# A Mamba-2 SSD stretch between two MLPs on one Trainium2 core: its order rewritten unit by unit, with steps moved between engines

## The chip, the cores and the metric

The kernel runs on one core of one Trainium2 chip. Its engines are TensorE (PE in the rows; PEld is its weight load), VectorE (DVE), ScalarE (ACT) and GpSimd (POOL), and SyncE (SP), whose queue issues nearly all DMAs. Each engine works through its own instructions in program order and meets the others at semaphores. The metric is the device time of one execution in microseconds.

## The reference, cut to what matters

512 tokens of width 1024 go through two layers: a pooling mixer with an MLP, then the SSD mixer with an MLP. The change touches the SSD mixer alone:

```python
zxbcdt = h @ w_in                       # z 2048, xBC 3072, dt 32
xbc = silu(causal_dwconv(xbc, conv_w, conv_b))      # 4 taps
dt = softplus(dt_raw + dt_bias); a = -exp(a_log)
# per group g of 4 (8 heads of 64, state 128), per chunk c of 128 tokens:
a_cs = cumsum(dt * a)
decay = exp(a_cs[l] - a_cs[s]) for s <= l
y_diag = (C B^T * decay) @ (x * dt)
y_off = (C @ state) * exp(a_cs);  state = state * exp(a_cs[-1]) + B^T @ (decay_to_end * x * dt)
y = (y_diag + y_off + d_skip * x) * silu(z)
y = y * rsqrt(mean over the group of y*y + eps) * norm_g
return y @ w_out
```

## The kernel before, in words

Activations lie feature-major: 128 features on the partitions, 512 tokens along them. Every large product is done in "units": one unit is a 1024 x 128 block of weights, eight weight tiles, and for each three matmuls of 512 columns (lines 696 to 698: high part by high, high by low, low by high), 24 in all, into one PSUM bank. A unit's weights are loaded by SP into one of two `w_raw` buffers; ACT rounds each half into `w_hi` (`round_half`, line 373) as soon as TensorE has used the same half of the unit two before; GpSimd subtracts (`split_half`, line 571) to get `w_lo`; SP may then load the unit after the next into `w_raw`. Two PSUM banks in turn are the accumulators.

The SSD stretch is 57 units. The first, a "slot" each from here on, gives the raw dt; six more give B, C and four x tiles of group 0. Then each group has ten slots t = 0 to 9: t = 0 to 3 are its four z tiles, t = 4 to 9 the six conv tiles (B, C, four of x) of the next group. In group 3, the slots from t = 4 on are the 16 units of the output projection instead; the first eight use groups 0 and 1, the last eight (from t = 12) groups 2 and 3.

Between units TensorE does the small matmuls of the group, at places fixed by tables: transposes of x and B and the products of C and B (`token_major`, lines 826, 829, 832) after t = 0, the four chunks (`chunk`, lines 845, 852, 858: diagonal part, state part, new state) after t = 2, 4, 6, 8 (2, 4, 5, 6 in group 3), the statistic of the previous group's squares (line 731) after t = 4 and its spread over the partitions by a product of ones and diagonals (line 738) after t = 5. In group 3 both are done once more at the end, the spread in the middle of the unit of slot t = 10.

On VectorE the conv of a tile is a load out of PSUM times the token's rstd (`conv_load`, line 1059, into `conv_in`), then four taps (lines 1073 and 1077), with Silu on ACT (line 477) behind them, tile by tile. The decay of a chunk is broadcast from DRAM into `m`; VectorE subtracts (line 1140) and limits (line 1146), ACT takes Exp (line 510), VectorE multiplies by the masked C B product (`decay_times_cb`, line 1153). Behind a chunk VectorE adds and decays y and state (lines 1162 to 1190). Of the group's norm VectorE does the diagonals (line 952, from `make_diagonals`, behind ACT's square root, line 403), the product with rstd and gain (line 1218) and the rounding (line 1226), GpSimd the sum of squares (line 645) and the residue (line 652). Elsewhere, in the MLPs, lines 1014 and 1018 are the square of the hidden tile and its residue.

The order on each engine is written out by hand in that engine's `group`; the tables say after which slot a thing comes:

```python
CHUNK_AFTER = {2: 0, 4: 1, 6: 2, 8: 3}
CHUNK_AFTER_LAST = {2: 0, 4: 1, 5: 2, 6: 3}
SEGMENT_AT = {0: 0, 2: 1, 4: 2, 6: 3}
T_GATE, T_SQ, T_STAT = 0, 1, 4
T_NORM, T_NORM_LAST = (6, 8), (6, 7)
```

## Time and profile before

| | |
|---|---|
| median of 3 runs | 1161.21 us (1160.94 to 1161.74) |
| span of the profiled execution | 1161.2 us |
| mean granted TensorE clock | 0.981 |
| TensorE, VectorE, ScalarE, GpSimd busy | 96%, 55%, 37%, 54% |
| SSD stretch, first unit of it to first unit of the second MLP | 379.4 to 797.3 us |
| starts of the groups' slots t = 0 | 422.9, 499.2, 578.3, 660.3 us |

The profiled execution's own time is its span, 1161.2 us. A row of the timeline gives start, length, engine, line, operation, output and inputs, and in brackets the idle time before it with what ended it. Instructions of one engine overlap a little, so that a length is longer than the distance to the next start.

### The profile page before, as it was taken

What the parts mean: (1) busy time and instruction counts of PE and PEld (TensorE: products, weight loads), DVE (VectorE), ACT (ScalarE), POOL (GpSimd) and SP (SyncE); (2) the same over time, 40 slices, a digit from 0 to 9 for tenths busy, and PEclk for the clock granted to TensorE, in tenths of its full rate; (3) what the DMA queues carried; (4) which work ended last, traced back from release to release, by engine and by line L of the source; (5) the groups of instructions that cost most, each with busy time, mean ns of one, the idle gap of its engine ahead of it and who ended that gap; (6) DMA issues with size and microseconds to landing.
All of it is one profiled execution on the core that took longest, in us unless ns stands there. A gap on an engine that the chain in (4) does not pass through costs nothing.

```text
span 1161.2 us, 15878 instructions
## 1 busy us (share of the span) xinstructions
PE 1118.9 (96%) x5142; PEld 915.8 (79%) x5142; DVE 637.0 (55%) x702; ACT 434.4 (37%) x670; POOL 622.8 (54%) x457
## 2 busy tenths in 40 slices
PE   9999999999999989999899799899999999999996
PEld 6788888888888778777677687688888888888885
DVE  6665422555322794987977978734565123564123
ACT  7334222233333355464455264233333222333331
POOL 4666444444566445356464563855665444554651
PEclk9999999999999999999899899899999999999998
DMA  6322322322322233333232223133222322322321
GB/s 249 109 90 96 103 90 90 108 90 91 108 90 90 91 114 109 118 102 120 80 126 94 96 91 100 60 104 103 96 90 94 105 90 94 105 90 94 106 90 72
DMA packets 39425, 117.35 MB, mean 101 GB/s; under 512 B 4065, under 2 KB 10721, under 8 KB 39393
## 3 DMA queue, kind: packets, MB, share of 16 engines
q1 hardware_dynamic: 39104, 116.21, 29.7%
q10 hardware_dynamic: 288, 0.73, 0.2%
q8 instruction: 18, 0.29, 0.1%
q14 instruction: 15, 0.11, 0.0%
HBM read 114.70 MB, written 2.23 MB: 101 GB/s over the span
## 4 chain that ended last, share of the span: by engine, by line
PE 82%; DVE 10%; issue 4%; ACT 2%; DMA 0%; DVEq 0%; POOL 0%; ACTq 0%
PE bank L696 26%; PE bank L697 26%; PE bank L698 26%; DVE tmp L1077 4%; DVE tmp L1073 1%; PE bank L845 1%; PE bank L826 1%; PE bank L852 1%; DVE conv_in L1059 1%; PE bank L858 1%; PE bank L754 1%; DVE squares L952 0%; DVE x_lo L920 0%; DMA x_token<-x_tok 0%; ACT x_hi L420 0%
## 5 line engine op out<-in xcount | busy, mean ns | idle before, releaser
L571 POOL TENSOR_TENSOR w_lo<-w_raw,w_hi 128x512 fp32r<-128x512 f32 x374 | 513.3, 1376 | 475.6 <-ACT w_hi L373 475.6
L373 ACT ACTIVATE w_hi<-w_raw 128x512 fp32r<-128x512 f32 x374 | 234.4, 628 | 450.9 <-PE bank L698 440.3
L696 PE MATMUL bank<-x_hi,w_hi 128*128 128x512 f32 x856 | 340.9, 398 | 2.6 <-DVE x_lo L920 1.9
L698 PE MATMUL bank<-x_hi,w_lo 128*128 128x512 f32 x856 | 333.8, 390 | 0.0
L697 PE MATMUL bank<-x_lo,w_hi 128*128 128x512 f32 x856 | 333.7, 390 | 0.0
L696 PE MATMUL bank<-act_hi,w_hi 128*128 128x512 f32 x640 | 252.6, 395 | 0.0
L698 PE MATMUL bank<-act_hi,w_lo 128*128 128x512 f32 x640 | 249.8, 390 | 0.0
L697 PE MATMUL bank<-act_lo,w_hi 128*128 128x512 f32 x640 | 249.8, 390 | 0.0
L696 PEld LDWEIGHTS bank<-x_hi,w_hi 128*128 128x128 f32 x856 | 161.3, 188 | 40.3 <-issue 5.7
L697 PEld LDWEIGHTS bank<-x_lo,w_hi 128*128 128x128 f32 x856 | 161.3, 188 | 35.8 <-issue 3.1
L698 PEld LDWEIGHTS bank<-x_hi,w_lo 128*128 128x128 f32 x856 | 161.0, 188 | 34.0
L1029 DVE TENSOR_TENSOR tmp<-bank,rstd 128x512 f32<-128x512 f32 x32 | 22.1, 692 | 240.5 <-PE bank L698 240.5
L696 PEld LDWEIGHTS bank<-act_hi,w_hi 128*128 128x128 f32 x640 | 120.7, 189 | 26.5 <-issue 1.0
L697 PEld LDWEIGHTS bank<-act_lo,w_hi 128*128 128x128 f32 x640 | 120.8, 189 | 26.3 <-issue 1.5
L698 PEld LDWEIGHTS bank<-act_hi,w_lo 128*128 128x128 f32 x640 | 120.6, 188 | 25.1
L1014 DVE TENSOR_TENSOR tmp<-tmp 128x512 f32<-128x512 f32 x64 | 116.1, 1814 | 2.2
L1011 DVE TENSOR_SCALAR tmp<-bank 128x512 f32<-128x512 f32 x64 | 44.3, 692 | 85.3 <-PE bank L698 85.3
L460 ACT ACTIVATE act_hi<-tmp 128x512 f32 x64 | 40.5, 632 | 122.0 <-DVE tmp L1014 122.0
L1018 DVE TENSOR_TENSOR act_lo<-tmp,act_hi 128x512 f32 x64 | 46.0, 719 | 59.0 <-ACT act_hi L460 59.0
L1077 DVE SCALAR_TENSOR_TENSOR tmp<-conv_in,params,tmp 128x512 f32<-128x512 f32 x72 | 72.8, 1010 | 2.5 <-DVE tmp L1073 0.2
L587 POOL TENSOR_TENSOR square_sum<-square_sum,squares 128x512 f32<-128x512 f32 x31 | 48.2, 1555 | 32.8 <-ACT squares L380 32.8
L1032 DVE TENSOR_TENSOR residual<-residual,tmp 128x512 f32 x32 | 53.6, 1674 | 4.9 <-DVE tmp L1029 2.5
(127 smaller groups left out, 713.3 us busy)
## 6 DMA issues: line engine op xcount, KB each, us to landing
w_raw<-weights SPq DMA_DIRECT2D x187, 512.0 KB, 3.3
m<-acs_scratch SPq DMA_DIRECT2D x16, 512.0 KB, 4.2
decay_in<-eacs_scratch SPq DMA_DIRECT2D x24, 128.0 KB, 3.4
x_token<-x_tok SPq DMA_DIRECT2D x4, 512.0 KB, 6.6
residual<-xt SPq DMA_DIRECT2D x8, 256.0 KB, 9.5
out_t<-scaled_residual SPq DMA_DIRECT2D x8, 256.0 KB, 2.3
pooling_matrices<-pooling ACTq DMA_DIRECT2D x1, 576.0 KB, 4.9
constants<-consts SPq DMA_DIRECT2D x1, 192.0 KB, 10.1
```

The lines of the kernel that those rows point to most:

```text
L373: act.activation(whi[:, c % 2, part], raw[:, c % 2, part], ACT.Copy).then_inc(hi_ready, 1)
L460: act.activation(act_hi[:, bass.ds(2 * i + e, 1), :], tmp[:, e:e + 1, :], ACT.Copy).then_inc(hid_hi_ready, 1)
L571: pool.tensor_tensor(wlo[:, c % 2, part], raw[:, c % 2, part], whi_f[:, c % 2, part], ALU.subtract).then_inc(lo_ready, 1)
L587: pool.tensor_tensor(ssq[:, :], ssq[:, :], sq[:, slot, :], ALU.add).then_inc(ssq_added, 1)
L696: pe.matmul(out, wh, xh, start=start, stop=False)
L697: pe.matmul(out, wh, xl, start=False, stop=False)
L698: return pe.matmul(out, wl, xh, start=False, stop=stop)
L1011: dve.tensor_scalar(tmp[:, e, :], acc[a % 2][:, :], 0.0, None, ALU.max).then_inc(acc_drained, 1)
L1014: dve.tensor_tensor(tmp[:, e, :], tmp[:, e, :], tmp[:, e, :], ALU.mult).then_inc(hid_sq_ready, 1)
L1018: dve.tensor_tensor(act_lo[:, tile, :], tmp[:, e:e + 1, :], act_hi_f[:, tile, :], ALU.subtract).then_inc(hid_lo_ready, 1)
L1032: dve.tensor_tensor(h[:, tile, :], h[:, tile, :], tmp[:, e:e + 1, :], ALU.add).then_inc(h_done, 1)
L1077: dve.scalar_tensor_tensor(out=out, in0=pre[:, k:k + TOK], scalar=col("conv_w", 24 * k + n), in1=out, op0=ALU.mult, op1=ALU.add).then_inc( ...
```

## The change

- The conv is done in the accumulator's bank: VectorE multiplies the bank by rstd in place (`conv_scale`), ACT does the last tap with the bias out of the bank (`first_tap`), VectorE the other three, reading the bank, into the B, C or x buffer (`conv_taps`). The `conv_in` buffer goes.
- Silu is done late and for many tiles at once: B, C, then z (four tiles) and x (four tiles) in slot t = 0 (`silu_b_c`, `silu_z`, `silu_x`); z of a group is activated in the next one.
- The decay exponent goes to ACT: eight Relus of 128 columns with the column of cumulated decays as bias, then Exp with scale -1. Lines 1140 and 1146 go.
- A third accumulator bank; bank 2 is no longer used for x tokens.
- The low part of the weights of the SSD stretch is made by VectorE (`ahead` there), from the third unit of the stretch to the last; GpSimd keeps the sum of squares and the decayed x. The residue of the normed y goes from GpSimd to VectorE (`norm_lo`), its rounding with the gain to ACT (`norm_hi`).
- Chunks come after t = 3, 5, 7, 9 (3, 4, 6, 7 in group 3); the transposes after t = 1, those of the fourth x chunk after t = 2; the statistic after t = 3; the spread after t = 5; at the end after t = 9 and t = 10. The loop over groups 1 and 2 is written out. In each slot every engine does `ahead` for the first half of the unit two ahead, then the slot's work, then the second half.

The core of the diff:

```diff
-CHUNK_AFTER = {2: 0, 4: 1, 6: 2, 8: 3}
-CHUNK_AFTER_LAST = {2: 0, 4: 1, 5: 2, 6: 3}
-SEGMENT_AT = {0: 0, 2: 1, 4: 2, 6: 3}
-SEGMENT_AT_LAST = {0: 0, 2: 1, 4: 2, 5: 3}
-T_GATE, T_SQ, T_STAT = 0, 1, 4
-T_NORM, T_NORM_LAST = (6, 8), (6, 7)
...
+CHUNK_AFTER = ({3: 0, 5: 1, 7: 2, 9: 3},) * 3 + ({3: 0, 4: 1, 6: 2, 7: 3},)
+T_TOKEN, T_LATE_TOKEN = 1, 2
+T_STAT, T_SPREAD = 3, 5
+T_STAT_END, T_SPREAD_END = 9, 10
...
+        acc3 = bank[0:3]
...
+        def lo_source(c, half, r=0):
+            if V_FROM <= c < V_TO:
+                return lo_v_ready, 2 * (c - V_FROM) + half + 1
+            return lo_ready, 2 * (c if c < V_FROM else c - (V_TO - V_FROM)) + half + 1 + 2 * r
...
+            def ahead(u, half):
+                round_half(U_SSM + u + 2, half)
...
+            def first_tap(n):
+                act.wait_ge(scaled, n + 1)
+                act.activation(conv_out(n), acc3[conv_slot(n) % 3][:, :], ACT.Identity,
+                               scale=col("conv_w", 24 * (CONV_K - 1) + n), bias=col("conv_b", n)
+                               ).then_inc(tap_ready, 1)
...
+            def silu_x(g):
+                act.wait_ge(acc_drained, A_SSM + conv_slot(CONVS * g + CONVS - 1) + 1)
+                act.activation(xact[:, :, :], xact[:, :, :], ACT.Silu).then_inc(x_act, 1)
...
             def exp_segments(g, c):
-                act.wait_ge(seg_ready, 4 * g + c + 1)
-                act.activation(mbuf[:, c % 2, :], mbuf[:, c % 2, :], ACT.Exp).then_inc(exp_done, 1)
+                act.wait_ge(m_landed[c % 2], 16 * (c // 2 + 1) + 32 * g)
+                for h in range(HPG):
+                    part = mbuf[:, c % 2, P * h:P * h + P]
+                    at_head = HEADS * c + HPG * g + h
+                    last = act.activation(part, part, ACT.Relu, scale=-1.0, bias=acs[:, at_head:at_head + 1])
+                last.then_inc(fall_ready, 1)
+                act.wait_ge(fall_ready, 4 * g + c + 1)
+                act.activation(mbuf[:, c % 2, :], mbuf[:, c % 2, :], ACT.Exp, scale=-1.0).then_inc(exp_done, 1)
...
+            def norm_hi(g):
+                for i in range(GT):
+                    act.wait_ge(yn_ready, GT * g + i + 1)
+                    act.activation(act_hi[:, GT * g + i, :], yx[:, GT * g + i, :], ACT.Copy,
+                                   scale=col("norm_g", GT * g + i)).then_inc(yhi_ready, 1)
...
+            for g in range(GROUPS):
+                ends = g == GROUPS - 1
+                for t in range(slots(g)):
+                    u = slot_of(g, t)
+                    ahead(u, 0)
                     if t == 0:
+                        silu_b_c(g)
+                        if g:
+                            silu_z(g - 1)
+                        silu_x(g)
+                    if t == 2:
+                        b_token(g)
+                        exp_segments(g, 0)
+                    if not ends and t == 8:
+                        exp_segments(g, 3)
+                    if ends and t == 6:
+                        exp_segments(g, 3)
+                    ahead(u, 1)
+                    if not ends and t >= GT:
+                        first_tap(CONVS * (g + 1) + t - GT)
+                    if t == 0:
+                        skip(g)
+                    if t == 1 and g:
+                        group_squares(g - 1)
+                    if t == 2:
+                        exp_segments(g, 1)
+                    if t == T_STAT + 1 and g:
+                        root(SSM_STAT + g - 1)
+                    if t == 5:
+                        exp_segments(g, 2)
+                    if t == T_SPREAD + 1 and g:
+                        norm_hi(g - 1)
+                    if ends and t == 7:
+                        silu_z(g)
+                    if ends and t == 8:
                         group_squares(g)
+                    if ends and t == T_STAT_END + 1:
                         root(SSM_STAT + g)
...
-            for j in range(7):
-                split_weights(U_SSM + 2 + j)
...
-            def y_residue(g, i):
-                pool.wait_ge(yhi_ready, GT * g + i + 1)
-                tile = bass.ds(GT * g + i, 1)
-                pool.tensor_tensor(act_lo[:, tile, :], yx[:, tile, :], act_hi_f[:, tile, :],
-                                   ALU.subtract).then_inc(ylo_ready, 1)
...
-            for m in range(KD):
-                split_weights(U_OUT + 8 + m + 2)
+            split_weights(U_MLP1)
+            split_weights(U_MLP1 + 1)
             mlp(U_MLP1, 3, 4)
...
+            def ssm_acc(u):
+                pe.wait_ge(acc_drained, A_SSM + u - (1 if u < 2 else 2))
+                return acc3[u % 3][:, :]
...
+                    if t == T_TOKEN:
+                        token_major(g)
+                    if t == T_LATE_TOKEN:
+                        pe.wait_ge(bt_ready, g + 1)
+                        token_x(g, CHUNKS - 1)
+                    if t == T_STAT and g:
                         pe.wait_ge(cbm_ready, g + 1)
+                        pe.wait_ge(ysum, (GT - 1) * g)
+                        statistic_by_token()
+                    if t == T_SPREAD and g:
                         spread(g - 1)
+                    if t in CHUNK_AFTER[g]:
+                        chunk(g, CHUNK_AFTER[g][t])
+                    if ends and t == T_STAT_END:
+                        pe.wait_ge(yn_ready, GT * g)
...
+            def ahead(u, half):
+                c = U_SSM + u + 2
+                if c >= V_TO:
+                    return
+                dve.wait_ge(hi_ready, 2 * c + half + 1)
+                part = slice(512 * half, 512 * half + 512)
+                dve.tensor_tensor(wlo[:, c % 2, part], raw[:, c % 2, part], whi_f[:, c % 2, part],
+                                  ALU.subtract).then_inc(lo_v_ready, 1)
+            def unit_done(u):
+                dve.wait_ge(wt_used, 2 * (U_SSM + u + 1))
+            def conv_scale(n):
+                p = acc3[conv_slot(n) % 3][:, :]
+                unit_done(conv_slot(n))
+                dve.tensor_tensor(p, p, rstd[:, :], ALU.mult).then_inc(scaled, 1)
+            def conv_taps(n):
+                p, out = acc3[conv_slot(n) % 3], conv_out(n)
+                dve.wait_ge(tap_ready, n + 1)
+                for k in range(CONV_K - 2, -1, -1):
+                    back = CONV_K - 1 - k
+                    if back > 1:
+                        dve.wait_ge(conv_step, 2 * n + back - 1)
+                    dve.scalar_tensor_tensor(out=out[:, back:], in0=p[:, 0:TOK - back],
...
-            def conv_load(g, q):
-                c, r, n = conv_place(g, q)
-                a = A_SSM + c - U_SSM
-                if c > U_SSM + 1:
-                    dve.wait_ge(conv_ready, n)
-                dve.wait_ge(wt_used, 2 * (c + 1) + 2 * r)
-                dve.tensor_tensor(pre[:, CONV_K - 1:], acc[a % 2][:, :], rstd[:, :], ALU.mult
...
-                    dve.tensor_scalar(out, pre[:, CONV_K - 1:], col("conv_w", 24 * k + n),
-                                      col("conv_b", n), ALU.mult, ALU.add).then_inc(conv_step, 1)
...
-            def segment_difference(g, c):
-                dve.wait_ge(m_landed[c % 2], 16 * (c // 2 + 1) + 32 * g)
-                m = by_head(mbuf[:, c % 2, :])
...
-            def segment_limit(g, c):
-                dve.wait_ge(seg_step, 4 * g + c + 1)
-                dve.tensor_scalar(mbuf[:, c % 2, :], mbuf[:, c % 2, :], 0.0, None, ALU.min).then_inc(seg_ready, 1)
...
+            def after_chunk(g, c):
                 if c == 0:
+                    dve.wait_ge(st_ready, 3 * g + 1)
+                    dve.tensor_copy(state[:, :], b_st[:, :]).then_inc(state_ready, 1)
                     dve.wait_ge(skip_ready, GT * g + GT)
+                    dve.wait_ge(yd_ready, 4 * g + 1)
+                    y = y_chunk(g, 0)
+                    dve.tensor_tensor(y, y, tiles(b_yd[:, :]), ALU.add).then_inc(y_add, 1)
+                    return
                 dve.wait_ge(yd_ready, 4 * g + c + 1)
                 y = y_chunk(g, c)
+                if c < CHUNKS - 1:
+                    dve.wait_ge(yo_ready, 3 * g + c)
+                    dve.tensor_tensor(by_head(state[:, :]), by_head(state[:, :]), of_group(cd, c, g, HD), ALU.mult
+                                      ).then_inc(h_step, 1)
+                dve.tensor_tensor(y, y, tiles(b_yd[:, :]), ALU.add).then_inc(y_add, 1)
+                if c < CHUNKS - 1:
+                    dve.wait_ge(st_ready, 3 * g + c + 1)
+                    dve.wait_ge(h_step, 2 * g + c)
+                    dve.tensor_tensor(state[:, :], state[:, :], b_st[:, :], ALU.add).then_inc(state_ready, 1)
                 dve.wait_ge(yo_ready, 3 * g + c)
+                dve.wait_ge(e_landed[c % 2], 32 * (2 * g + (c == 3) + 1) if c % 2 else 32 * (g + 1))
                 dve.tensor_tensor(tiles(ytmp[:, :]), tiles(b_yo[:, :]), e2[:, c % 2, :, :], ALU.mult
+                                  ).then_inc(y_dec, 1)
+                dve.wait_ge(y_add, 4 * g + c + 1)
+                dve.wait_ge(y_dec, 3 * g + c)
                 dve.tensor_tensor(y, y, tiles(ytmp[:, :]), ALU.add).then_inc(y_done, 1)
...
+            def norm_lo(g, i):
+                dve.wait_ge(yhi_ready, GT * g + i + 1)
+                dve.scalar_tensor_tensor(out=act_lo[:, GT * g + i, :], in0=yx[:, GT * g + i, :],
+                                         scalar=col("norm_g", GT * g + i), in1=act_hi_f[:, GT * g + i, :],
+                                         op0=ALU.mult, op1=ALU.subtract).then_inc(ylo_ready, 1)
...
+            for g in range(GROUPS):
+                ends = g == GROUPS - 1
+                chunk_after = CHUNK_AFTER[g]
+                for t in range(slots(g)):
+                    u = slot_of(g, t)
+                    ahead(u, 0)
+                    if t == 0 and g:
+                        after_chunk(g - 1, CHUNKS - 1)
+                    if t == 1 and g:
+                        gate(g - 1)
+                    if t == 2:
+                        masked_cb(g)
+                        token_x(g, 0)
+                        token_x(g, 1)
+                        token_x(g, 2)
+                    if t == 3:
+                        token_x(g, 3)
+                    if t == T_STAT + 1 and g:
+                        token_mean(g - 1)
+                    if t and t - 1 in chunk_after:
+                        after_chunk(g, chunk_after[t - 1])
+                    if chunk_after.get(t) in (2, 3):
+                        decay_times_cb(g, chunk_after[t])
+                    if ends and t == 8:
+                        gate(g)
+                    if ends and t == T_STAT_END + 1:
+                        token_mean(g)
+                        make_diagonals(SSM_STAT + g)
+                    if ends and t == T_SPREAD_END + 1:
+                        norm_y(g)
+                    if t < GT:
+                        gate_in(g, t)
+                    elif ends:
+                        add_output(t - GT)
+                    else:
+                        conv_scale(CONVS * (g + 1) + t - GT)
+                    ahead(u, 1)
+                    if not ends and t >= GT:
+                        conv_taps(CONVS * (g + 1) + t - GT)
+                    if t == 2:
+                        decay_times_cb(g, 0)
+                    if t == 3:
+                        decay_times_cb(g, 1)
+                    if t == T_STAT + 1 and g:
+                        make_diagonals(SSM_STAT + g - 1)
+                    if t == T_SPREAD + 1 and g:
+                        norm_y(g - 1)
+                    if t in (T_SPREAD + 2, T_SPREAD + 3) and g:
+                        norm_lo(g - 1, 2 * (t - T_SPREAD - 2))
+                        norm_lo(g - 1, 2 * (t - T_SPREAD - 2) + 1)
+                    if ends and t == T_SPREAD_END + 1:
+                        for i in range(GT):
+                            norm_lo(g, i)
             for m in range(KD):
+                ahead(slot_of(GROUPS - 1, GT + 8 + m), 0)
                 add_output(KD + m)
+                ahead(slot_of(GROUPS - 1, GT + 8 + m), 1)
                 residue(3, m)
             mlp(U_MLP1, A_MLP1, 32, 6, None)
```

## Rows read from the trace of the kernel before

**Rows 1.** The page, its first part: busy time and share of each engine, whole span.
```profile
PE 1118.9 (96%) x5142; PEld 915.8 (79%) x5142; DVE 637.0 (55%) x702; ACT 434.4 (37%) x670; POOL 622.8 (54%) x457
```

**Rows 2.** Busy time by stretch: start and end, length, then busy us (instructions) by engine.
```profile
100.00:300.00 200.00, 200.00 (x882) 165.30 (x881) 87.53 (x78) 57.78 (x95) 101.52 (x77) 1.00 0.29 96
...
499.20:578.30 79.10, 72.57 (x373) 58.62 (x372) 65.01 (x82) 39.84 (x54) 43.20 (x28) 0.96 0.31 105
...
379.40:797.30 417.90, 390.38 (x1916) 315.95 (x1915) 310.71 (x376) 190.94 (x263) 227.02 (x156) 0.96 0.30 100
```

**Rows 3.** Who TensorE waited for from 379.4 to 797.3 us: total, times, longest.
```profile
PE bank L845 <- DVE y_accumulated L1175: 11.7, 6, 4.3
PE bank L826 <- ACT x_conv L477: 10.5, 4, 3.4
PE bank L738 <- DVE squares L952: 3.2, 1, 3.2
PE bank L810 <- DVE a_dt L1109: 1.4, 1, 1.4
PE bank L845 <- DVE m L1153: 0.3, 1, 0.3
PE bank L803 <- DVE tmp L1044: 0.2, 1, 0.2
```

**Rows 4.** The six stretches of low clock, same view: the first, and the sum.
```profile
430.45:437.27 6.82, 5.38 (x25) 5.38 (x26) 5.64 (x8) 2.67 (x5) 1.62 (x2) 0.50 0.54 210
...
sum 34.13, PE 29.49 PEld 26.14 DVE 29.92 ACT 7.93 POOL 8.77; mean PE 4.91 PEld 4.36 DVE 4.99 ACT 1.32 POOL 1.46
```

**Rows 5.** Timeline of TensorE's small matmuls: start, length, idle before and its releaser.
```profile
431.89 3.68 PE L826 MATMUL bank<-constants,x_conv 128*128 128x128 f32 x16 [3.40 <-ACT x_conv L477]
...
506.37 1.96 PE L826 MATMUL bank<-constants,x_conv 128*128 128x128 f32 x16 [1.54 <-ACT x_conv L477]
...
586.79 3.07 PE L826 MATMUL bank<-constants,x_conv 128*128 128x128 f32 x16 [2.85 <-ACT x_conv L477]
...
461.62 1.09 PE L845 MATMUL bank<-m,x_dt 128*64 128x128 f32 x16
...
463.64 1.02 PE L858 MATMUL bank<-x_dt_decayed,b_token 128*128 128x512 f32 x2
...
533.45 0.95 PE L731 MATMUL bank<-constants,square_sum 128*128 128x1 f32 x8
```

**Rows 6.** Durations by line: min/median/max in ns, first and last start.
```profile
L373 ACT ACTIVATE w_hi<-w_raw x374: 612/632/659, 11.8 to 1135.7; 128x512 fp32r<-128x512 f32 x187
L510 ACT ACTIVATE m<-m x16: 1057/1062/1066, 438.4 to 710.7; 128x1024 f32<-128x1024 f32 x16
L645 POOL TENSOR_TENSOR square_sum<-square_sum,squares x8: 1277/1292/2162, 524.5 to 732.8; 128x512 f32<-128x512 f32 x8
L1014 DVE TENSOR_TENSOR tmp<-tmp x64: 1161/1824/1827, 36.7 to 1060.2; 128x512 f32<-128x512 f32 x64
L1018 DVE TENSOR_TENSOR act_lo<-tmp,act_hi x64: 691/694/804, 38.8 to 1063.0; 128x512 f32 x64
L1153 DVE TENSOR_TENSOR m<-m,cb_masked x16: 1211/1224/2314, 439.5 to 714.2; 128x1024 f32<-128x1024 f32 x16
```

**Rows 7.** Timeline of VectorE: runs of like instructions, start and length of the run.
```profile
508.34 2.48 DVE L1196 TENSOR_TENSOR x_dt<-bank,dt_token 128x512 f32<-128x512 f32 x4
...
394.05 2.33 DVE L1077 SCALAR_TENSOR_TENSOR tmp<-conv_in,params,tmp 128x512 f32<-128x512 f32 x3
...
539.61 0.88 DVE L952 TENSOR_SCALAR squares<-constants,rstd_token 128x128 f32<-128x128 f32 x4
```

**Rows 8.** Timeline of ScalarE: a table load and the activations behind it.
```profile
415.85 1.28 ACT L503 ACT_TABLE_LOAD   x1
417.14 0.31 ACT L503 ACTIVATE decay_to_end<-decay_to_end 128x128 f32<-128x128 f32 x1
417.36 0.29 ACT L504 ACTIVATE chunk_decay<-cumulated 128x128 f32<-128x128 f32 x1
```

More of the change, by code:

```diff
@@ L682, in _ @@
-            group(0, 0, first=True)
-            with pool.Fori(1, GROUPS - 1) as g:
-                group(g, PER_GROUP * g)
-            group(GROUPS - 1, PER_GROUP * (GROUPS - 1), last=True)
+                                       ALU.add).then_inc(ysum, 1)
+            pool.wait_ge(decays, 1)
+            for g in range(GROUPS):
+                if g:
+                    group_sum(g - 1)
+                for c in range(CHUNKS - 1):
+                    decayed(g, c)
+            group_sum(GROUPS - 1)
@@ L805, in _ @@
-            for j in (2, 3):
-                unit(U_SSM + j, 0, accumulator(A_SSM + j), xhi, xlo, 0)
-            pe.wait_ge(adt_ready, 1)
-            flat = adt[:, :, :].rearrange("p c h -> p (c h)")
-            pe.matmul(b_stat[:, 0:P], upper, flat, start=True, stop=True)
-            pe.matmul(b_stat[:, P:2 * P], ones, flat, start=True, stop=True)
-            for c in range(CHUNKS):
-                last = pe.matmul(bank[2][0:HEADS, P * c:P * c + P], adt[:, c, :], upper, start=True, stop=True)
```

635 lines of the change are left out of this document (240 added, 395 removed).

## The prediction

> **What bounds the kernel now.** I read the page first: TensorE is busy 96% of the span, the other engines at most 55% [rows 1]. Then stretches of time. Away from the SSD stretch TensorE never pauses: 882 matmuls in 200 us [rows 2], 0.227 us each, so a unit of 24 takes 5.44 us. The SSD stretch runs from 379.4 to 797.3 us, 417.9 us for 57 units. These need 57 x 5.44 = 310.1 us, so 107.8 us are something else, and only this can change. The waits of TensorE in it name 11.7 + 10.5 + 3.2 + 1.4 + 0.3 + 0.2 = 27.3 us [rows 3]. The granted clock is at its lower level (0.5, that is 1.2 GHz) in six stretches of 34.1 us in all [rows 4]; some 4.4 us of them lie inside the stops, where no matmul could run, so the matmuls lose (34.1 - 4.4) / 2 = 14.9 us, 2.5 us per stretch. What is left, 107.8 - 27.3 - 14.9 = 65.6 us, is the small matmuls (transposes, chunks, statistics). The first low stretch began at 430.4, inside the stop of 3.40 us that ended at 431.9; after a stop of 2.85 us there was one too; the stop of 1.54 us that ended at 506.4 had none [rows 4, 5].
>
> So the time is TensorE's own order, plus its stops, plus the clock after them: 310.1 + 65.6 + 27.3 + 14.9. VectorE is busy 65 of the 79 us of group 1 [rows 2]: it has room, but it works in a fixed order, and each stop is a result that came late through its queue or ACT's.
>
> **Parts without a price of their own.** TensorE gets the same matmuls in other places: 65.6 us stays. The third accumulator bank takes away no stop, since no row of the waits is for an accumulator. Batched Silu and paired Exp save table loads of 1.28 us [rows 8] on an engine with room; a load counts only where the walk below meets it. The weights' low part, a GpSimd instruction so far, becomes a VectorE instruction like the one of 0.69 us [rows 6]. With GpSimd nearly idle (six instructions a group are left) VectorE seldom meets the 1.82 us that a like instruction took beside GpSimd [rows 6]. I take 0 for meetings that remain; the other end is 1 us per group, in slot 2, where GpSimd's sums fall. The moved DMAs (decay broadcasts, at most four transfers in a slot) are issued behind a chunk and used two or more slots later; weight loads still start a full unit before ACT reads them: no price.
>
> **The walk.** I go through the slots queue by queue. Prices: VectorE starts a 512-column instruction each 0.60 us (four in 2.48), three taps take 2.33, four diagonals 0.88 [rows 7]; m times CB 1.22, a half of w_hi 0.63, the Exp of a chunk 1.06, a sum on GpSimd 1.29 [rows 6]. An activation of 128 columns takes 0.31, but 0.2 from start to start [rows 8], so a chunk's eight Relus are 1.7 to 2.5 us; I take 2.0. Not in the trace is a VectorE instruction that writes PSUM in place (`conv_scale`): lower end 0.60, upper 0.79 (a tap, with its wait for the tap before); I take 0.60, since its sources are those of the old conv_in. On TensorE the second and third chunk take 3.0, the first 2.1 and the fourth 2.4 with a part less each, a statistic 0.9, a spread 1.0, the 16 transposes 2.0 [rows 5]. ACT is released 3.0 us into a unit for its first half and 5.6 for its second.
>
> *Slots 0 to 5, groups 1 and 2.* Slot 0 on ACT: w_hi, Silu load, B and C, z and x in one instruction of four tiles each: x is done 9.9 us in, and TensorE asks for it at about 12.4. Slot 2: w_hi, b_token, Relus, Exp load, Exp, w_hi, then VectorE: m of chunk 0 is ready 25.7 us after the group began, asked for at 26.1. The spread after slot 5 finds its diagonals 0.4 us early. No stop: the transposes' 10.5 us [rows 3] go, with 0.4 us to spare at the closest.
>
> *Slot 6.* Counted from its start: w_hi to 3.6, w_lo to 4.3, `after_chunk(1)`, five instructions, to 7.4, `conv_scale` 8.1, the first tap on ACT 8.9, three taps to 11.2, `norm_y` four to 13.6, ACT's `norm_hi` to 14.4. Only now comes ACT's first half of w_hi of slot 7 (15.0), its w_lo (15.6), and behind it on VectorE `decay_times_cb(2)`: 16.9. TensorE is through unit 7 at 10.9. A stop of **6.0 us** in groups 1 and 2. Group 0 has no norm here: 13.0, a stop of 2.1.
>
> *Slots 8 and 9.* From slot 8's start: w_lo 4.3, `after_chunk(2)` 7.4, scale 8.0, first tap 8.9, taps 11.2, two `norm_lo` 12.5, w_lo of slot 9 13.1, `decay_times_cb(3)` 14.3, asked for at 10.9: **3.5 us**; group 0, without the norm, again 2.1. These new waits are queue order: ahead of a late m stand taps and norm of other tiles.
>
> *Group 3.* Chunk 1: `y_add` 0.3 late. Chunk 2: its Exp ends behind a table load, then w_hi, w_lo, m: 1.5. Chunk 3, after slot 7: w_lo 4.3, `after_chunk(2)` 7.4, m 8.7, asked for at 5.4: 3.2. The squares' sum after slot 9: gate done 8.8 us after slot 8 began, three sums on GpSimd to 12.5, asked for at 10.9: 1.7. The spread after slot 10: ACT's root stands behind the second half of w_hi of that slot, so nothing of it runs before the unit ends: 0.2 + 0.63 + load 1.28 + root 0.2 + reciprocal and diagonals 1.1, 3.5 us (the old one waited 3.2 [rows 3]). The last residues: 0.5. Together 10.7.
>
> *Prologue.* VectorE now carries 14 halves of w_lo beside conv and softplus series. Each comes up to a slot later than GpSimd's, still in time; the series ends 0.6 us after it is asked for (1.4 now), the dt tile 0.3 (0.2 now): 0.9. If VectorE fell further behind here, TensorE would wait for w_lo itself.
>
> **The sum.** Waits 0.9 + 4.2 + 2 x 9.5 + 10.7 = 34.8. Stops over 2.85 us: two in each of groups 1 to 3, six at 2.5 us of clock, 14.9 as now. 310.1 + 65.6 + 34.8 + 14.9 = 425.4 against 417.9: **+7.5 us**. The profiled execution's span is 1161.2; the median of the three runs is 1161.21, so the two agree and nothing lies around the span. 1168.7, rounded **1169**: what the transposes no longer wait for comes back in two later stops per group, and the last group adds its own.
>
> **Bounds.** Low: the eleven stops shorter by 1 us each, and two of them not followed by a low clock: -11 - 5, 1153. High: Relus at 0.31 (0.4 in each of four groups after the margin, 0.8 at group 3's chunk 2: +2.4), GpSimd beside VectorE (+1 in three groups), `conv_scale` at 0.79 (+0.2 at six stops), group 0's two stops lowering the clock (+5): +11.6, 1180. The forecast's own range is 1164 to 1180.
>
> **Rivals.**
> *A. Faster: the stops of slots 6 to 9 half covered (23%).* Place: m of chunks 2 and 3. My chain of fourteen steps adds every handover, and 0.2 us too much in each is 3 us. Then most stops stay under 2.85 us and the clock stays up. Against: each step has its row, and the order is fixed. Price: half of 34.8 and two low stretches, 310.1 + 65.6 + 17.4 + 5 = 398.1, 1141; halfway from there to the forecast, 1155. I give it 1148. It decides at m of chunk 2 ready before 14 us after slot 6 begins.
> *B. Faster: all covered (4%).* Only sub-microsecond waits, some 6 us: 381.7, 1125. It needs the norm off slot 6's chain, where the code has it.
> *C. No change (10%).* Within 0.2% (2.3 us, about what a measurement of this kernel can tell). One of groups 1 and 2 loses its stop of 3.5 us with the 2.5 us of clock behind it: -6, 1163.
> *D. Slower still: a table switch costs more than its load (5%).* In the trace the next activation starts at the load's end, 417.14 after 415.85 + 1.28 [rows 8]. If as much again were lost at each switch ahead of an Exp or root that TensorE awaits: chunk 0 +1.0 in four groups, spread +1.0 in three, chunk 2 +0.2 twice and +1.4 once, last root +1.4: +10, 1179. The Trainium skill has such a rule ("ScalarE: Activation LUTs", What ACT_TABLE_LOAD costs): about 1283 ns of load and 1380 ns of drain at every switch. By that rule the result is rival D's; the trace agrees with the load and shows no drain.
> *E. The forecast (58%).* That the change does not do what it says I give nothing: in the diff each moved instruction has its own new counter, and no old one is left to wait for.
>
> Faster is A and B, 27%; same C, 10%; slower D and E, 63%. **The range**, 1146 to 1180, leaves out B, the lower half of A, and what may lie above D.
>
> **What would show it.** Right: no wait over 1 us at the transposes of x; the largest waits are for m by `decay_times_cb`, 6 us twice, 3.5 twice, 3.2 once; 3.5 us for the diagonals of the last spread; about 34 us of low clock; the SSD stretch about 425 us. Wrong: m of chunk 2 awaited under 3 us in groups 1 and 2, or an SSD stretch under 415 us; a TensorE wait for w_lo (then VectorE's pace bounds the kernel and I missed it); a wait for an accumulator; low-clock stretches outside the SSD stretch that are not there now.

## The result, and the profile after

The changed kernel takes **1170.74 us** (median of 4 runs, 1168.32 to 1171.72) against 1161.22 for the kernel before (4 runs beside it). The ratio is 1.0082, 95% interval 1.0067 to 1.0096: 9.5 us slower, where 1169 was forecast. The profiled execution has a span of 1169.9 us, 8.7 more than before's.

The page of the changed kernel, its first part, and from the costliest groups the instruction that moved to VectorE:

```profile
PE 1120.3 (96%) x5142; PEld 916.4 (78%) x5142; DVE 615.3 (53%) x765; ACT 465.8 (40%) x793; POOL 434.4 (37%) x330
...
L1081 DVE TENSOR_TENSOR w_lo<-w_raw,w_hi 128x512 fp32r<-128x512 f32 x110 | 81.6, 744 | 105.5 <-ACT w_hi L380 105.3
```

By shares nothing is wrong. GpSimd fell by 188 us against [rows 1], VectorE by 22 even with 81.6 us of w_lo added, and TensorE is at 96% as before. The end of the w_lo row matters more: VectorE stood idle 105.5 us in front of these 110 instructions, waiting for ScalarE's rounding.

Busy time by stretch, changed kernel (start and end, length, then busy us and instructions on PE, weight load, VectorE, ScalarE, GpSimd, then granted clock, DMA share and GB/s): a stretch away from the SSD part, the SSD stretch, groups 0 and 1, and group 3 with the output projection:

```profile
100.00:300.00 200.00, 200.00 (x883) 165.22 (x882) 87.94 (x79) 57.96 (x96) 101.54 (x77) 1.00 0.29 97
...
379.77:806.01 426.24, 392.29 (x1915) 316.74 (x1914) 288.81 (x439) 221.73 (x386) 38.33 (x30) 0.95 0.30 98
421.61:496.00 74.39, 70.28 (x363) 56.72 (x362) 50.98 (x75) 39.87 (x74) 3.25 (x3) 0.96 0.41 126
496.00:580.20 84.20, 74.92 (x375) 60.55 (x374) 60.30 (x92) 47.68 (x84) 7.77 (x6) 0.93 0.30 101
...
662.29:806.01 143.72, 132.64 (x624) 106.92 (x624) 82.82 (x127) 69.77 (x116) 16.78 (x13) 0.96 0.26 88
```

The first line is that of [rows 2] again: 8.3 of the 8.7 us lie in the SSD stretch, 426.2 us against 417.9; the other 0.4 lie ahead of it. Group 1 takes 84.2 us (79.1 before), with 5 us less work on VectorE.

Who TensorE waited for between 370 and 850 us (total, times, longest), changed kernel:

```profile
PE bank L880 <- DVE m L1190: 27.3, 8, 5.9
PE bank L750 <- DVE squares L986: 3.4, 1, 3.4
PE bank L743 <- POOL square_sum L691: 2.5, 1, 2.5
PE bank L711 <- DVE act_lo L1246: 0.4, 1, 0.4
```

Against [rows 3] the transposes' 10.5 us and the 11.7 for y are gone, and one wait stands in their place: m, the product of `decay_times_cb`, 27.3 us in eight stops. In order of time they are 2.05 and 2.05 (group 0), 5.89 and 3.38 (group 1), 5.89 and 3.38 (group 2), 1.49 and 3.12 (group 3).

The stretches of low clock (granted clock 0.5, that is 1.2 GHz) in the SSD part of the changed kernel, TensorE alone: the first, the first of group 1, the last, and the sum of all nine:

```profile
477.06:480.48 3.42, 3.42 (x10) 0.50 0.80 284
...
555.57:562.40 6.83, 6.01 (x28) 0.50 0.45 148
...
753.54:756.96 3.42, 3.01 (x5) 0.50 0.23 75
sum 40.99, PE 35.69; mean PE 3.97
```

Nine stretches and 41.0 us, where six and 34.1 stood in [rows 4].

The stop of 5.89 us ends at 556.39, when m is there. VectorE before it, changed kernel, timeline (start, length, instruction, idle before and its releaser); slot 6 of group 1 begins on TensorE at 539.01:

```profile
543.10 0.69 DVE L1081 TENSOR_TENSOR w_lo<-w_raw,w_hi 128x512 fp32r<-128x512 f32 x1 [3.46 <-ACT w_hi L380]
543.71 0.68 DVE L1207 TENSOR_TENSOR state<-state,chunk_decay 128x512 f32<-128x512 f32 x1
...
546.29 0.69 DVE L1220 TENSOR_TENSOR y_accumulated<-y_accumulated,y_tmp 128x512 f32<-128x512 f32 x1
546.90 0.69 DVE L1091 TENSOR_TENSOR bank<-bank,rstd 128x512 f32<-128x512 f32 x1
547.50 0.68 DVE L1081 TENSOR_TENSOR w_lo<-w_raw,w_hi 128x512 fp32r<-128x512 f32 x1
548.45 2.31 DVE L1101 SCALAR_TENSOR_TENSOR x_conv<-bank,params,x_conv 128x511 f32<-128x511 f32 x3 [0.26 <-ACT x_conv L489]
550.68 2.47 DVE L1241 TENSOR_TENSOR y_accumulated<-y_accumulated,bank 128x512 f32<-128x512 f32 x4
554.51 0.69 DVE L1081 TENSOR_TENSOR w_lo<-w_raw,w_hi 128x512 fp32r<-128x512 f32 x1 [1.36 <-ACT w_hi L380]
555.12 1.22 DVE L1190 TENSOR_TENSOR m<-m,cb_masked 128x1024 f32<-128x1024 f32 x1
```

ScalarE in the same kernel and stretch (same columns):

```profile
539.66 1.28 ACT L548 ACT_TABLE_LOAD   x1
540.95 1.06 ACT L548 ACTIVATE m<-m 128x1024 f32<-128x1024 f32 x1
542.43 0.63 ACT L380 ACTIVATE w_hi<-w_raw 128x512 fp32r<-128x512 f32 x1 [0.42 <-PE bank L713]
...
551.39 2.56 ACT L559 ACTIVATE act_hi<-y_accumulated,params 128x512 fp32r<-128x512 f32 x4 [2.98 <-DVE y_accumulated L1241]
553.86 1.14 ACT L380 ACTIVATE w_hi<-w_raw 128x512 fp32r<-128x512 f32 x2
```

The Exp that m needs ended at 542.0. The multiplication came 13 us later, because it stands in slot 7, behind all that VectorE has to do in slot 6. At the start of the slot that order is held 3.46 us by a w_lo that waits for ScalarE. Then come five instructions of `after_chunk`, the convolution of another tile and the norm of another group. At 553.15 VectorE stops again for 1.36 us, for the w_hi of the *next* slot, which ScalarE has queued behind `norm_hi`.

### The profile page after: what moved, and what is told of

It is laid out like the page before. It is cut to its first block, busy times and chain, and to the rows that moved or that the text cites. A ratio compares the mean times of both kernels' runs of the same rounds, so it can differ in the third digit from the quotient of the medians.

```text
span 1169.9 us, 15307 instructions
## 1 busy us (share of the span) xinstructions
PE 1120.3 (96%) x5142; PEld 916.4 (78%) x5142; DVE 615.3 (53%) x765; ACT 465.8 (40%) x793; POOL 434.4 (37%) x330
## 4 chain that ended last, share of the span: by engine, by line
PE 86%; DVE 7%; ACT 4%; issue 2%; DMA 0%; POOL 0%; DVEq 0%; ACTq 0%; POOLq 0%
PE bank L711 27%; PE bank L712 26%; PE bank L713 26%; PE bank L880 2%; PE bank L889 1%; PE bank L897 1%; ACT w_hi L380 1%; DVE x_conv L1101 1%; DVE m L1190 1%; ACT act_hi L559 1%; PE bank L839 1%; PE bank L766 1%; DVE w_lo L1081 0%; DVE x_lo L962 0%; DMA x_token<-x_tok 0%
## 5 line engine op out<-in xcount | busy, mean ns | idle before, releaser
L619 POOL TENSOR_TENSOR w_lo<-w_raw,w_hi 128x512 fp32r<-128x512 f32 x264 | 350.6, 1331 | 355.3 <-ACT w_hi L380 355.3
L1081 DVE TENSOR_TENSOR w_lo<-w_raw,w_hi 128x512 fp32r<-128x512 f32 x110 | 81.6, 744 | 105.5 <-ACT w_hi L380 105.3
L691 POOL TENSOR_TENSOR square_sum<-squares 128x512 f32<-128x512 f32 x4 | 6.2, 1551 | 247.6 <-ACT squares L553 247.6
L635 POOL TENSOR_TENSOR square_sum<-square_sum,squares 128x512 f32<-128x512 f32 x31 | 48.3, 1558 | 32.6 <-ACT squares L387 32.6
```

The costliest lines, as they stand in the source:

```text
L619: pool.tensor_tensor(wlo[:, c % 2, part], raw[:, c % 2, part], whi_f[:, c % 2, part], ALU.subtract).then_inc(lo_ready, 1)
L635: pool.tensor_tensor(ssq[:, :], ssq[:, :], sq[:, slot, :], ALU.add).then_inc(ssq_added, 1)
L1081: dve.tensor_tensor(wlo[:, c % 2, part], raw[:, c % 2, part], whi_f[:, c % 2, part], ALU.subtract).then_inc(lo_v_ready, 1)
```

## The experiments

The theory was the forecast's: TensorE stops because awaited results stand behind others in VectorE's fixed order. The rival: VectorE is given more in slots 2 to 9 than it can do in time, in whatever order, the low part of the weights above all. In the diffs + is what the kernel has instead of the changed one. The kernel before took 1161.22 us beside the first four runs (median of 19), 1161.05 beside the next four and 1161.58 beside the last three (11 each).

**One step earlier at a time.**

In e1 the product of chunk 2 in groups 0 to 2 stands in slot 6, right behind `ahead(u, 0)`:

```diff
                     ahead(u, 0)
...
+                    if not ends and t == 6:
+                        decay_times_cb(g, 2)
...
-                    if chunk_after.get(t) in (2, 3):
+                    if chunk_after.get(t) == 3 or (ends and chunk_after.get(t) == 2):
```

e2 does the same for chunk 3, in slot 8 ahead of `conv_taps`:

```diff
                     ahead(u, 1)
+                    if not ends and t == 8:
+                        decay_times_cb(g, 3)
...
-                    if chunk_after.get(t) in (2, 3):
+                    if chunk_after.get(t) == 2 or (ends and chunk_after.get(t) == 3):
```

e3 puts `after_chunk` ahead of the first half of w_lo:

```diff
                     u = slot_of(g, t)
-                    ahead(u, 0)
                     if t == 0 and g:
                         after_chunk(g - 1, CHUNKS - 1)
+                    if t and t - 1 in chunk_after:
+                        after_chunk(g, chunk_after[t - 1])
+                    ahead(u, 0)
```

> One line moved in the changed kernel: in groups 0 to 2 the product of m and CB of chunk 2 is done in slot t = 6, behind the low part and ahead of the chunk's sums, instead of in t = 7. Theory (queue order): its Exp is done 3 us into slot 6, so the stops of 2.05, 5.89 and 5.89 us at chunk 2 go, and with them about 7 us of low clock: near 1150 us, TensorE waits for m near 13 us in all. Rival (VectorE has too much to do; the lateness only moves on): the same time within 3 us, and the 14 us turn up at chunk 3, at w_lo or at an accumulator.

> One line moved in the changed kernel: in groups 0 to 2 the product of m and CB of chunk 3 is done in slot t = 8 ahead of the taps, instead of in t = 9. Theory (queue order): Exp of chunk 3 ends some 8 us after slot 8 began, m is ready 1 us before TensorE asks; the stops of 2.05, 3.38 and 3.38 us go, with about 6 us of low clock: near 1156 us; the stops at chunk 2 stay at 2.05, 5.89, 5.89. Rival (too much work on VectorE): within 3 us of 1170.7, with longer stops at chunk 2 or at w_lo.

> In every slot VectorE does the sums behind a chunk before the low part of the first half, not after it. It sits idle there for about 3 us, since the first half of w_hi is released 3 us into the unit. Theory (queue order): each chain of slots 6 to 9 begins up to 3 us earlier but then meets the end of the unit at 5.6 us: stops at chunk 2 of groups 1 and 2 near 4 us instead of 5.9, at chunk 3 near 1.6 instead of 3.4, group 0's under 0.5, group 3's chunk 3 near 1: about 12 us of stops and 4 us of clock less, near 1155 us. Rival (too much work): no more than 3 us faster.

Measured: 1159.91 (ratio to before 0.9986, 0.9976 to 0.9995), 1158.11 (0.9975, 0.9966 to 0.9985) and 1152.93 (0.9922, 0.9905 to 0.9939). That is 10.8, 12.6 and 17.8 us under the changed kernel. TensorE waited for m 18.4 us in five stops in e2 and 18.1 in eight in e3, the longest 5.9 and 4.1. In e1 it was:

```profile
PE bank L880 <- DVE m L1190: 22.2, 5, 7.8
```

e2 and e3 came about 2 us from what the theory expected. e1 gave only half of its 20.7 us, and more than the rival's 3. The stops at chunk 2 are gone there (8 became 5), but the stop at chunk 3 grew from 3.38 to 7.76 us in groups 1 and 2. The reason is on VectorE in e1, timeline of slots 8 and 9 of group 1:

```profile
556.64 1.41 DVE L1246 SCALAR_TENSOR_TENSOR act_lo<-y_accumulated,params,act_hi 128x512 fp32r<-128x512 f32 x2
557.96 0.69 DVE L1081 TENSOR_TENSOR w_lo<-w_raw,w_hi 128x512 fp32r<-128x512 f32 x1
...
566.85 0.69 DVE L1081 TENSOR_TENSOR w_lo<-w_raw,w_hi 128x512 fp32r<-128x512 f32 x1
567.45 1.22 DVE L1190 TENSOR_TENSOR m<-m,cb_masked 128x1024 f32<-128x1024 f32 x1
```

The same place of the changed kernel, the first w_lo of slot 8 (in e1 it starts at 557.96):

```profile
565.79 0.69 DVE L1081 TENSOR_TENSOR w_lo<-w_raw,w_hi 128x512 fp32r<-128x512 f32 x1 [4.35 <-ACT w_hi L380]
```

There VectorE had caught up while TensorE stood still at chunk 2, and then waited 4.35 us for ScalarE. In e1 it comes to slot 8 without a pause, and the stop at chunk 3 is 4.38 us longer. So a stop taken away is in part handed to the next late result.

**The weights' low part back on GpSimd, alone.**

`ahead` issues nothing on VectorE; GpSimd has the two halves in each slot, with its own steps between them:

```diff
-V_FROM, V_TO = U_SSM + 2, U_MLP1
+V_FROM, V_TO = UNITS, UNITS
...
+                    split_half(c, 0)
+                    if t == 2:
+                        decayed(g, 0)
+                        decayed(g, 1)
...
+                    split_half(c, 1)
```

> The changed kernel with the low part of the weights back on GpSimd, in the new order; the decayed x and the sums of squares stand between the halves on GpSimd. Theory (queue order): VectorE's queue loses the low part of slot 7 that stands between the norm and m of chunk 2, so this stop falls from 5.9 to between 3 and 4 us and that of chunk 3 from 3.4 to between 2 and 3, and VectorE's instructions with two operands in SBUF take longer beside GpSimd (1.8 us instead of 0.7 for some): near 1166 us, between 1160 and 1172. Rival (VectorE's amount of work is what costs): 12 us a group of work leave it, stops at m vanish, under 1155 us. Second rival (the port is what costs): slower than 1172 us.

1146.80 us (0.9877, 0.986 to 0.9893), 23.9 under the changed kernel. My theory had said 1160 to 1172 and the rival under 1155, so this run stood for the rival. The waits for m (the lines of the program have moved by ten and four):

```profile
PE bank L890 <- DVE m L1194: 9.8, 7, 2.1
```

VectorE's timeline of the same place shows what has gone:

```profile
539.79 0.70 DVE L1095 TENSOR_TENSOR bank<-bank,rstd 128x512 f32<-128x512 f32 x1 [2.69 <-PE bank L723]
541.34 2.32 DVE L1105 SCALAR_TENSOR_TENSOR x_conv<-bank,params,x_conv 128x511 f32<-128x511 f32 x3 [0.85 <-ACT x_conv L489]
543.57 2.47 DVE L1245 TENSOR_TENSOR y_accumulated<-y_accumulated,bank 128x512 f32<-128x512 f32 x4
545.96 1.22 DVE L1194 TENSOR_TENSOR m<-m,cb_masked 128x1024 f32<-128x1024 f32 x1
```

Between the norm and m there were 0.69 us of w_lo and 1.36 us of waiting for ScalarE in the changed kernel; now there is nothing. With w_lo out of the queue, `after_chunk` no longer waits for the rounding either. This would explain the gain by order as well: three w_lo stand ahead of this m in the changed kernel, and the first and the last wait 3.46 and 1.36 us for w_hi. To part the two readings, w_lo had to be on VectorE in a good order.

**All orders together, with w_lo on either engine.**

e5 is e1 and e2 together. e6 and e7 put every awaited result first. On VectorE in each slot (the + lines stood behind the first half of w_lo so far):

```diff
+                    if ends and t == T_STAT_END + 1:
+                        token_mean(g)
+                        make_diagonals(SSM_STAT + g)
+                    if t == 0 and g:
+                        after_chunk(g - 1, CHUNKS - 1)
+                    if t and t - 1 in chunk_after:
+                        after_chunk(g, chunk_after[t - 1])
+                    if ends and t == 8:
+                        gate(g)
+                    if ends and t == T_SPREAD_END + 1:
+                        norm_y(g)
                     ahead(u, 0)
+                    if not ends and t == 6:
+                        decay_times_cb(g, 2)
```

Chunk 3's product stands in slot 8 as in e2. Both kernels also have one more wait in `after_chunk`, for VectorE's own sum of the chunk before (`y_done`). In the last group ScalarE has root, squares and `norm_hi` ahead of the rounding and the exponents of chunks 2 and 3 in slots 4 and 5, and VectorE their products in slots 5 and 6. e7 leaves w_lo on VectorE; e6 has it on GpSimd, as e4, but with the last group's sum of squares one slot earlier.

> Both products m of groups 0 to 2 ahead: chunk 2's in slot 6, chunk 3's in slot 8 ahead of the taps. Alone the first took 10.8 us from the changed kernel (1159.9), the second 12.6 (1158.1). If only the place in VectorE's order counts, the two add up and the m waits fall to about 5 us in all, with 1145 to 1149. If VectorE is late as a whole in slots 6 to 9, the stop at chunk 3 stays at some 3.6 us in groups 1 and 2, the m waits hold 10 to 14 us, and the time is 1149 to 1153; I take 1150.

> What a conversion chunk, both products, the last group's exponents, root, diagonals and normalisation each waited for is put ahead of them on VectorE and ScalarE, and the weights' low part is back on GpSimd. Order and load both at fault: TensorE's stops in the SSD stretch fall under 5 us, no low clock there, 1124 to 1130. If the units themselves slow down once the stops go (an accumulator not drained in time, a landing late), 1135 to 1145, with new waits of TensorE on the accumulators.

> The kernel e6 with the weights' low part on VectorE, as the change has it: 110 subtractions, 81.6 us of it, back on that engine. If the load was costly only because the awaited steps stood last in each slot, it costs nothing once they stand first: within 3 us of e6. If VectorE lacks the time in slots 2 to 9 whatever the order, 6 to 15 us above e6, with waits for w_lo or m of over 1 us each.

e5 took 1145.76 us (0.9868, 0.9853 to 0.9883), e6 1126.92 (0.9702, 0.9688 to 0.9715), e7 **1120.45** (0.9648, 0.9635 to 0.9661). e5 is 25.0 under the changed kernel, a little more than its two halves singly (10.8 + 12.6). Its time is that of the first reading, but 11.1 us of waits for m stay, as the second had it: in groups 1 and 2 each stop at chunk 3 is 3.25 us, VectorE being late as a whole there. (These waits are of its profiled execution, which took 1150.36 us; the other three took 1145.7 to 1145.8.) All waits of TensorE in the SSD stretch of e6:

```profile
PE bank L753 <- POOL square_sum L691: 2.0, 1, 2.0
PE bank L721 <- DVE act_lo L1252: 0.7, 1, 0.7
PE bank L760 <- DVE squares L996: 0.5, 2, 0.2
PE bank L890 <- DVE m L1194: 0.5, 2, 0.2
```

And of e7, then its SSD stretch by windows:

```profile
PE bank L880 <- DVE m L1190: 0.6, 2, 0.3
```

```profile
379.82:754.77 374.95, 374.11 (x1916) 303.91 (x1914) 287.68 (x439) 221.27 (x386) 38.55 (x30) 1.00 0.33 112
```

The rival falls here. VectorE does the same 287.7 us of work as in the changed kernel (288.8) in a stretch that is 51 us shorter, and TensorE is busy 374.1 of 375.0 us at full clock. w_lo on VectorE costs nothing in this order; it is even 6.5 us *better* than on GpSimd, where "within 3 us" was expected. The profiled SSD stretches differ by 7.5 us (382.49 against 374.95). The stops of e6 (3.7 us, 0.6 in e7) and its one stretch of low clock, 6.8 us at half speed, make 3.1 + 3.4 = 6.5 of it. The largest stop of e6, 1.97 us, is again a matter of order: on GpSimd the last sums of squares start at 697.74, right behind a half of w_lo of 1.83 us. With a better place for them e6 might come near e7; this was not tried. The same move thus costs 23.9 us in one order and gains 6.5 in another, as these two orders have it. VectorE in e7, timeline of slot 6, group 1:

```profile
532.07 0.68 DVE L1207 TENSOR_TENSOR state<-state,chunk_decay 128x512 f32<-128x512 f32 x1
...
534.65 0.69 DVE L1222 TENSOR_TENSOR y_accumulated<-y_accumulated,y_tmp 128x512 f32<-128x512 f32 x1
535.61 0.69 DVE L1081 TENSOR_TENSOR w_lo<-w_raw,w_hi 128x512 fp32r<-128x512 f32 x1 [0.27 <-ACT w_hi L380]
536.22 1.22 DVE L1190 TENSOR_TENSOR m<-m,cb_masked 128x1024 f32<-128x1024 f32 x1
537.60 0.70 DVE L1091 TENSOR_TENSOR bank<-bank,rstd 128x512 f32<-128x512 f32 x1 [0.17 <-PE bank L713]
```

`after_chunk` now runs while ScalarE rounds, so w_lo waits 0.27 us instead of 3.46, and m comes 4.2 us after the slot's first instruction, not 12.

**The last group's end.**

Its root on ScalarE and its mean and diagonals on VectorE, each ahead of that engine's part of the weights:

```diff
+                    if ends and t == T_STAT_END + 1:
+                        root(SSM_STAT + g)
                     ahead(u, 0)
...
+                    if ends and t == T_STAT_END + 1:
+                        token_mean(g)
+                        make_diagonals(SSM_STAT + g)
...
                     ahead(u, 0)
```

> Only the last group's end: its root on ScalarE ahead of the rounding of the next unit's weights, token mean and diagonals on VectorE ahead of the first half of w_lo. The stop before the normalisation's spread (3.36 us in the changed kernel) falls under 1 us; with the 3.4 us of low clock behind it 4 to 5 us are gained: 1166. If the stop is set by ScalarE's square root and its table load of 1.28 us rather than by the queue ahead, only 1 us is gained: 1170.

1165.24 us (ratio to before 1.0035, 1.0023 to 1.0047), 5.5 under the changed kernel; the wait for the diagonals is gone from the list and its stretch of low clock with it. In the profiled execution the stretch behind group 0's first stop of 2.05 us is missing as well (3.4 us at half speed, so 1.7), which this edit can't account for; part of the 5.5 may not be its own. e5, e3 and e8 together hold every reorder of groups 0 to 2 and the spread. Their gains sum to 25.0 + 17.8 + 5.5 = 48.3 us, near the 50.3 between the changed kernel and e7; no run has just these three together, so that they add up is not shown.

**Parts of the change undone in the good order.** With the stops away, three parts could be asked for their own worth. Each is e7 with one part as it was. e9, two accumulator banks:

```diff
-                pe.wait_ge(acc_drained, A_SSM + u - (1 if u < 2 else 2))
-                return acc3[u % 3][:, :]
+                pe.wait_ge(acc_drained, A_SSM + u - 1)
+                return acc3[u % 2][:, :]
```

e10, the exponent on VectorE in place of ScalarE's eight Relus (chunk 0 in slot 1, chunk 1 in slot 2, chunks 2 and 3 in slots 5 and 7; in the last group 4 and 5):

```diff
+                dve.tensor_tensor(m, m, of_group(acs, c, g, P), ALU.subtract).then_inc(seg_step, 1)
+                dve.wait_ge(seg_step, 4 * g + c + 1)
+                dve.tensor_scalar(mbuf[:, c % 2, :], mbuf[:, c % 2, :], 0.0, None, ALU.min).then_inc(seg_ready, 1)
```

e11, one tile of z in each of slots 1 to 4:

```diff
-                z = zs[:, GT * g:GT * g + GT, :]
+                z = zs[:, GT * g + i, :]
```

> The kernel e7 (1120.5) with two accumulator banks in the SSD stretch in place of three; b_c and x of a unit now have one unit, not two, until the bank is needed. In e7 the convolution of a unit is out of its bank 3.8 us after VectorE takes it, inside the next unit (5.4 us and more); only behind the softplus chain, 5.7 us on VectorE near 402 to 408 us, is one late, by 1 to 2 us. So 1121 to 1123 with one stop on the accumulator; if the third bank carries the change, every chunk slot would stop for 2 us or more, nine stops and 1140 or above.

> The kernel e7 with the decay exponent on VectorE as in the kernel before: 16 subtractions and 16 limits come to it (42.5 us in the kernel before, 1628 and 1025 ns each), 128 small activations (39.2 us) leave ScalarE. In e7 VectorE is busy without a gap worth the name in slots 5 to 9, and the exponents of chunks 2 and 3 fall there, 2.7 us each: if that backlog reaches m, 2 to 3 us at two chunks of three groups and low clock behind them, 1130 to 1140. If slack of two units takes it up, 1120 to 1123. I take 1128.

> The kernel e7 with the gate's Silu in four operations of 512 columns as each tile comes, in place of one of 2048: it alternates with the exponentials, so some 12 to 16 more table loads of 1.28 us stand on ScalarE, 15 to 20 us of its time. ScalarE waits most of the time in these slots: within 1 us of e7. If a table load in front of an exponent or a rounding is what a stop starts from, 2 to 8 us above, with waits for m or w_hi.

e9: 1122.93 us (0.9667, 0.9655 to 0.968), 2.5 over e7, with the one stop on the accumulator behind the softplus chain:

```profile
PE bank L711 <- DVE x_conv L1101: 1.2, 1, 1.2
```

So the third bank is worth 2 to 3 us in this order, as expected. e11: 1123.88 us (0.9675, 0.9662 to 0.9687), 3.4 over e7, not the 1 at most that was held likelier, but within its other range of 2 to 8: ScalarE has 12 activations and 8 table loads more (11.1 us, fewer loads than reckoned), and TensorE six short stops of 0.35 to 0.63 us. e10: 1150.87 us (0.9905, 0.989 to 0.992), 30.4 over e7, where 8 were expected. The waits of TensorE in e10's SSD stretch, then chunk 0's Exp on ScalarE and what VectorE does until chunk 0's product, slots 2 and 3 of group 1:

```profile
PE bank L875 <- DVE m L1193: 19.4, 6, 4.2
```

```profile
511.60 1.06 ACT L543 ACTIVATE m<-m 128x1024 f32<-128x1024 f32 x1 [2.70 <-DVE m L1185]
...
514.48 2.08 DVE L1183 TENSOR_TENSOR m<-m,cumulated 128x1024 f32<-128x1024 f32 x1
516.60 0.69 DVE L1185 TENSOR_SCALAR m<-m 128x1024 f32<-128x1024 f32 x1
...
518.41 1.22 DVE L1193 TENSOR_TENSOR m<-m,cb_masked 128x1024 f32<-128x1024 f32 x1
```

The six stops are three of 4.2 us at chunk 0's product in groups 1 to 3 (519.68, 600.09, 682.28), two of 3.4 at chunk 3's in groups 1 and 2, and one of 0.2. The expectation had stops of 2 to 3 us at the late chunks only. At chunk 0 the Exp is done at 512.66, but the product starts at 518.41, and VectorE does not pause between. The exponent of chunk 1 (514.48 to 517.29) stands among what it does first. With the stops comes low clock: TensorE is busy 1112.4 us, 10.8 more than in e7, for the same matmuls. Whether the exponents could be put in better places on VectorE was not tried, so 30 us is the price of this placement, and how much of it is the work's own is open.

## Why the prediction came out right

**The sum.** The mechanism came out as forecast: the transposes stopped nothing, and m, late in VectorE's order, did. Forecast 310.1 + 65.6 + 34.8 + 14.9 = 425.4 us for the SSD stretch, measured 426.2. The floor of 310.1 + 65.6 = 375.7 us is what e7 runs at: 374.95, 0.6 of it stops. The waits are 27.3 + 3.4 + 2.5 + 0.4 = 33.6 by the list. What is left of the 426.2 beside e7's 374.4 and these waits is 18.2 us: low clock (35.7 us of matmul time at half speed, which makes 17.8) and stops too short for the list. So the floor came out 1.3 us lower than forecast (374.4 for 375.7), the waits 1.2 lower and the rest 3.3 higher. That these nearly cancel is luck; the sum is closer than its terms. The forecast's own working has two small slips: 34.13 - 29.49 of [rows 4] is 4.6 us of low clock inside the stops and not 4.4, and the walk has ten stops of 1 us or more, where the low bound counts eleven.

**The walk**, forecast and measured, us:

| stop | forecast | measured |
|---|---|---|
| chunk 2, groups 1 and 2 | 6.0 | 5.89, 5.89 |
| chunk 3, groups 1 and 2 | 3.5 | 3.38, 3.38 |
| group 0, both | 2.1 | 2.05, 2.05 |
| group 3: chunks 2 and 3 | 1.5, 3.2 | 1.49, 3.12 |
| squares' sum | 1.7 | 2.54 |
| last spread | 3.5 | 3.36 |
| last residues | 0.5 | 0.42 |

The queues walked gave each stop of m to 0.12 us. `conv_scale`, the one price that no row had, starts the next instruction 0.60 us after itself (546.90, 547.50), as taken. The eight Relus take 2.45 us, the upper end and not 2.0; at chunk 3 the Exp was done before it was wanted, so it cost nothing.

**What was mis-sized.** *The squares' sum:* "three sums on GpSimd" at 1.29 us. They took 4.90 (1.55 alone, then two in 3.21). GpSimd, changed kernel:

```profile
737.37 1.55 POOL L691 TENSOR_TENSOR square_sum<-squares 128x512 f32<-128x512 f32 x1 [44.63 <-ACT squares L553]
739.06 3.21 POOL L691 TENSOR_TENSOR square_sum<-square_sum,squares 128x512 f32<-128x512 f32 x2
```

*The prologue and chunk 1 of group 3:* 0.9 and 0.3 were taken, no wait over 0.1 is there. *The clock,* the largest error: "stops over 2.85 us, six at 2.5". There were nine stretches of 41.0 us, where six and about 34 were the forecast's own sign. Both of group 0's stops of 2.05 us lowered the clock, as did that of 2.54. The upper bound had group 0's two, nothing had the third. The length was off the other way: six of the nine last 3.4 us and three 6.8, where the mean of before was 5.7. The two errors leave 17.8 against 14.9.

**The price of zero.** "I take 0 for meetings that remain" is about VectorE being slowed beside GpSimd, and no stop in slots 0 to 5 came of it. The w_lo instruction itself stands in the walk only as a step of each chain, with the wait for ScalarE that precedes it. Taking it away in the changed kernel's order gives 23.9 us (e4), more than any one step moved alone (e1, e2, e3, e8), while in e7's order it costs nothing. The prediction never said so. A reader of it would have looked for the loss in the norm and the taps.

**The rivals.** A (half covered): no, the handovers were not overcounted; all three stops of chunk 2 are as long as walked. B (all covered, 1125) named what it needs, "the norm off slot 6's chain"; e7 does that and more and lands at 1120. C (no change): no, the change costs 9.5 us, and both stops of 3.4 us with their low clock are there. D, a table switch that costs more than its load: the Exp starts at 540.95, the end of the load (539.66 + 1.28), and the last root at 752.57 behind its load of 1.28 at 751.27. Nor is there a pause ahead of these loads: the instructions before them end at 539.64 and 751.25. The Trainium skill ("ScalarE: Activation LUTs", What ACT_TABLE_LOAD costs) adds a drain of 1380 ns to the load; the load of 1283 ns agrees with these rows, the drain does not appear in them.

## What to carry to other kernels

An instruction moved to an engine with room brings its own wait along: everything behind it in that engine's order now waits for its source too. Price a move by walking the queue and asking what stands behind it, not by its duration; here the same move was worth 6.5 us of gain in one order and 23.9 of loss in another. When a stop is found, put what it waits for right behind the last thing that it needs, and do it at all such places at once, since one alone hands part of its lateness to the next; putting the awaited results first gave 50 us, where rewriting the stretch had lost 9.

## What the runs showed of the hardware

- The same stop did not always lower the clock. In e4 there are four stops for m of 2.04 to 2.06 us; behind two of them (563.26 and 639.05) TensorE's granted clock was 0.5 for 3.4 us, behind the others (547.24 and 623.03) it stayed at 1.0. In the changed kernel both of 2.05 lowered it, and the stop of 1.49 did not. In e8 the first of these two, at the same place and as long (475.75), left it at 1.0.
- VectorE's product of 128x1024 took 1218 ns on average in the changed kernel (none over 1221) and 1438 in e6, where GpSimd works on w_lo beside it: there half of them took 1224 or less, and the longest 2316. GpSimd's own w_lo took 1349 ns on average in e6, against VectorE's 744 for the same operation in the changed kernel.
